# Up-projection of a hybrid decoder layer: weight sums T1, T3 and T4 of chunks 1 and 2 formed by accumulating transfers instead of on VectorE

## The reference

```
def conv_glu_ffn(h, w_up, conv_w, conv_b, w_down):
    u = h @ w_up                      # (512, 2048) @ (2048, 2 * 5632)
    c = causal_depthwise_conv(u, conv_w, width 3) + conv_b
    gate, val = jnp.split(c, 2, axis=-1)
    return (jax.nn.gelu(gate, approximate=True) * val) @ w_down
```

## Time and profile before

| | us |
|---|---|
| median of 3 runs | 2002.81 |
| lowest, highest | 2002.68, 2005.13 |
| profiled execution, its own time | 2000.05 |
| its span | 1998.1 |
| TensorE busy | 1966.3 (98%) |
| VectorE busy | 1475.0 (74%) |
| ScalarE busy | 1012.6 (51%) |
| GpSimd busy | 55.1 (3%) |

### The profile page before, as it was taken

How to read it: one execution, slowest core, us unless ns; L and a number is a source line. 1 busy time by engine, 2 the same in 40 slices (tenths; PEclk the granted TensorE clock), 3 DMA queues, 4 the chain that set the end, 5 groups by cost and what they waited for, 6 DMA issues and landing times.

```text
span 1998.1 us, 27810 instructions
## 1 busy us (share of the span) xinstructions
PE 1966.3 (98%) x10408; PEld 1678.4 (84%) x10408; DVE 1475.0 (74%) x2044; ACT 1012.6 (51%) x1539; POOL 55.1 (3%) x65
## 2 busy tenths in 40 slices
PE   8999999999999999999999999999999999999998
PEld 6888888888887889888888888888889887888786
DVE  4343544445436899788888888888888998889888
ACT  6442323435435764555555555555555655555454
POOL 0000000000000000000000000000000000000000
PEclk9999999999999999999999999999999999999999
DMA  9462322221646534777877787887786997877675
GB/s 383 147 223 94 102 90 64 85 64 64 241 133 200 185 121 162 195 194 209 230 198 198 216 228 192 205 227 210 200 207 193 310 323 233 276 244 242 214 265 202
DMA packets 229108, 388.02 MB, mean 194 GB/s; under 512 B 11842, under 2 KB 139970, under 8 KB 219120
## 3 DMA queue, kind: packets, MB, share of 16 engines
q1 hardware_dynamic: 219520, 320.19, 47.8%
q0 software_dynamic: 8208, 59.77, 14.9%
q10 hardware_dynamic: 1248, 6.29, 0.8%
HBM read 286.30 MB, written 44.07 MB: 165 GB/s over the span
## 4 chain that ended last, share of the span: by engine, by line
PE 85%; DVE 9%; issue 2%; ACT 2%; DMA 0%; DVEq 0%; ACTq 0%
PE ring L2514 15%; PE ring L2270 13%; PE ring L2272 12%; PE ring L2271 12%; PE ring L2516 8%; PE side L2514 7%; PE side L2516 3%; DVE w_lo L1906 3%; PE side L2270 3%; PE side L2271 2%; PE side L2272 2%; PE side L2346 1%; PE side L2319 1%; DVE f L2116 1%; PE side L2329 1%
## 5 line engine op out<-in xcount | busy, mean ns | idle before, releaser
L1605 DVE TENSOR_TENSOR w_lo<-raw,w_hi 128x512 fp32r<-128x512 f32 x256 | 169.5, 688 | 270.5 <-ACT w_hi L1122 270.3
L2514 PE MATMUL ring<-s,w_hi 128*128 128x512 f32 x864 | 306.2, 397 | 2.3 <-ACT snaps L1441 2.2
L1906 DVE TENSOR_TENSOR w_lo<-raw,w_hi 128x1024 fp32r<-128x1024 f32 x216 | 253.3, 1173 | 74.4 <-ACT w_hi L1332 55.9
L1906 DVE TENSOR_TENSOR w_lo<-q,w_hi 128x1024 fp32r<-128x1024 f32 x218 | 255.4, 1172 | 44.0 <-ACT w_hi L1332 27.1
L1122 ACT ACTIVATE w_hi<-raw 128x512 fp32r<-128x512 f32 x256 | 151.1, 622 | 198.2 <-PE ring L2272 193.8
L2516 PE MATMUL ring<-s,w_lo 128*128 128x256 f32 x864 | 242.0, 280 | 0.0
L1332 ACT ACTIVATE w_hi<-q 128x1024 fp32r<-128x1024 f32 x176 | 185.1, 1055 | 51.6 <-PE side L2516 46.0
L2514 PE MATMUL ring<-a,w_hi 128*128 128x512 f32 x576 | 202.6, 396 | 0.0
L2270 PE MATMUL ring<-w_hi,act_hi 128*128 128x512 f32 x488 | 193.0, 395 | 9.2 <-DVE w_lo L1605 8.7
L2514 PEld LDWEIGHTS ring<-s,w_hi 128*128 128x128 f32 x864 | 162.0, 188 | 44.3 <-ACT snaps L1441 6.2
L1332 ACT ACTIVATE w_hi<-raw 128x1024 fp32r<-128x1024 f32 x130 | 135.1, 1056 | 112.4 <-DVE raw L1609 78.4
(11 more groups left out here) (331 smaller groups left out, 4360.0 us busy)
## 6 DMA issues: line engine op xcount, KB each, us to landing
q<-in_w_up SPq DMA_DIRECT2D x65, 1024.0 KB, 5.4
raw<-in_w_in SPq DMA_DIRECT2D x24, 1024.0 KB, 5.2
raw<-in_w_up SPq DMA_DIRECT2D x23, 1024.0 KB, 8.3
q<-q POOLq DMA_DIRECT2D x19, 1024.0 KB, 6.9
q<-raw POOLq DMA_DIRECT2D x19, 1024.0 KB, 6.9
raw<-q POOLq DMA_DIRECT2D x19, 1024.0 KB, 7.3
q<-in_w_down SPq DMA_DIRECT2D x66, 256.0 KB, 4.7
raw<-in_w_down SPq DMA_DIRECT2D x66, 256.0 KB, 4.4
```

The lines of the kernel that those rows point to most:

```text
L1605: dve.tensor_tensor(w_lo[:, s, q], raw[:, s, q], w_hi[:, s, q].bitcast(F32), ALU.subtract).then_inc(lo_done, 1)
L1906: dve.tensor_tensor(lo, src, hi.bitcast(F32), ALU.subtract).then_inc(hp_lo_done, 1)
L2514: pe.matmul(bank.rearrange("p (h n) -> p h n", h=2), b_hi, hi_lo, start=first, stop=False, skip_group_check=True)
```

## The change

`PAIRED` keeps its meaning for the products. A new constant `ADDED = 1` takes its place where the sums are concerned: from chunk 1 on, T1, T3 and T4 are accumulating transfers, so six additions of 128 x 2048 leave VectorE and six 1 MB transfers join GpSimd's queue. T2 of chunk 1 stays in `after(14)`; T2 of chunk 2 moves from `after(27)`, behind that window's remainder, to `after(28)`, ahead of it. Waits for T1, T3 and T4 of chunks 1 and 2 (`t_ready`) now name the transfers' semaphores, and so does SyncE's wait for T4 of chunk 1 ahead of the load of b11 of chunk 3.

```
+ADDED = 1
 def t_count(c, name):
-    if c < PAIRED[0]:
-        order = ("T1", "T3", "T2", "T4") if c == 0 else ("T1", "T2", "T3", "T4")
+    if c < ADDED:
+        order = ("T1", "T3", "T2", "T4")
         return 4 * c + order.index(name) + 1
-    return 4 * PAIRED[0] + c - PAIRED[0] + 1
+    return 4 * ADDED + c - ADDED + 1
 def t_ready(c, name):
-    if c >= PAIRED[0] and name != "T2":
-        return {"T1": t1_in, "T3": t3_in, "T4": t4_in}[name], 16 * (c - PAIRED[0] + 1)
+    if c >= ADDED and name != "T2":
+        return {"T1": t1_in, "T3": t3_in, "T4": t4_in}[name], 16 * (c - ADDED + 1)
...
-            for c in range(PAIRED[0], CHUNKS):
+            for c in range(ADDED, CHUNKS):
                 pool.wait_ge(hp_lo_done, place(c, P1, 1) + 1)
                 pool.wait_ge(*b_landed("12", c))
                 pool.dma_start(b11_at(c)[:, :, :].rearrange("p k n -> p (k n)"),
                                b12_at[:, :, :].rearrange("p k n -> p (k n)"), accum_op=ALU.add).then_inc(t1_in, 16)
                 pool.wait_ge(*b_landed("22", c))
-                pool.wait_ge(t1_in, 16 * (c - PAIRED[0] + 1))
+                pool.wait_ge(t1_in, 16 * (c - ADDED + 1))
                 pool.dma_start(b12_at[:, :, :].rearrange("p k n -> p (k n)"),
                                raw[:, 0, :], accum_op=ALU.add).then_inc(t3_in, 16)
...
                 if w == 14:
                     make_t(1, "T2")
-                if PAIRED[0] <= c < CHUNKS and s == 0:
+                if ADDED < c < CHUNKS and s == 0:
                     make_t(c, "T2")
...
-                if w == 13:
-                    make_t(1, "T1")
-                if w == 16:
-                    make_t(1, "T3")
...
-                    if s == 5 and c < PAIRED[0]:
+                    if s == 5 and c < ADDED:
                         make_t(c, "T4")
-                    if c == 1 and s in (12, 13):
-                        make_t(c + 1, ("T1", "T2")[s - 12])
-                    if c == 2 and s == 0:
-                        make_t(c, "T3")
```

## The result

The changed kernel takes 2007.44 us (median of 16 runs, 2005.0 to 2012.24); the kernel before, run beside it, 2002.96 us (16 runs, 2000.57 to 2005.64). The ratio is 1.0025, with a 95% interval from 1.0018 to 1.0032: 4.5 us slower, where +3.2 us was forecast. The interval leaves no doubt that the kernel is slower. The time is inside the forecast's range. Run again among the experiments, the same kernel gave 1.0033 and 1.0025.

What follows compares the result with a forecast made beforehand. TensorE, busy 98% of the span, was taken to bound the kernel. The terms +1.4 + 1.7 - 0.3 + 0.4 gave +3.2 us, so 2002.81 + 3.2 = 2006.0 us, range 2001.2 to 2008.0.

Steps and rivals of the forecast that it cites:

- What can be won: Chunks 1 and 2: TensorE loses 2.3 us in all at products 18, 20 and 34, the most the change can gain.
- T2 of chunk 1, "+1.4 us, by the row of a real meeting": Ahead of product 18: T1's transfer and b22's load slow each other, so T2 starts near 732.05, 1.4 us later.
- The upper end, +2.0: Ahead of product 18: b22's load served only behind T1 lands at 732.5, T2 starts at 732.65, 2.0 us later.
- The clock, +1.7: At product 18: a 3.0 us wait brings TensorE's clock to half speed for about 3.4 us, losing 1.7 us.
- Product 20, -0.3: Chunk 1: with T3 off VectorE the combination is done some 2 us earlier, gaining 0.3 us.
- Product 34, +0.4: Chunk 2: between 0.3 us gained and 1.2 lost if spilled sums push T1 back; the middle, 0.4 us lost.
- T3 and T4 of both chunks at nothing: Chunks 1 and 2: these transfers land before their first users need them, costing nothing.
- The transfers hide: Chunk 1: T1 and b22's load do not slow each other; sum -1.5 us, 2001.3 us; chance 10%.
- the clock stays up: Product 18: its longer wait brings no fall of the clock; sum +1.5 us, 2004.3 us; chance 22%.
- VectorE holds GpSimd's transfers up: Issue of T1: VectorE's additions delay the transfer's preparation by up to 2.3 us; sum +5.5, 2008.3 us; chance 3%.
- Served one after the other: Chunks 1 and 2: meeting transfers queue whole, b22 behind T1, T1 behind spills; sum +4.6, 2007.4 us; chance 18%.
- Same, 74%: Whole kernel: 74% chance that the time stays within 0.2%, 4.0 us, of the kernel before.

Runs made afterwards that it cites:

- the kernels that have only the good half of the change: Changed kernel with T1 of chunk 1, or of chunks 1 and 2 (two forms), back on VectorE: ratio 1.0000, and 0.9995 and 0.9997.
- first profile: The changed kernel as first measured and profiled, against the kernel before: 2007.44 us, ratio 1.0025.
- third: The changed kernel run once more without edit, the later of two repeats: 2007.57 us, ratio 1.0025.
- chunk 1 alone: Changed kernel with all four sums of chunk 2 on VectorE, transfers only in chunk 1: 2008.3 us, ratio 1.0029.
- with filling matmuls: Changed kernel with 24 further matmuls between products 17 and 18 into a free bank: 2008.66 us, ratio 1.0025.
- second: The changed kernel run once more without edit, the earlier of two repeats: 2009.23 us, ratio 1.0033.

## Why the prediction was off

The direction, the range and the path by which T2's delay reaches TensorE were right. One term was too small, and the picture of the meeting behind it was wrong.

The forecast took the earlier trace rows as two transfers that share the engines and lose 2.1 us each. The list of DMA queues of the kernel before, from 1136 to 1141.5 and from 1141.5 to 1144.6, says otherwise:

```profile
q0 software_dynamic: 128, 1.05, 99.9%
...
q1 hardware_dynamic: 988, 1.00, 92.2%
```

The load, issued at 1139.80, moved nothing until all of T4 was through. By the usual microsecond from issue to first data it could have begun near 1140.8, so T4 cost it only some 0.7 us; at product 18 the load lost over 2 us in the same way. The rest of its 7.0 us is its end: from 1144.8 to 1146 the engines were busy by a share of 0.07, as at the late b12 above. T4's landing after 9.4 us came 3 us after its last data, and why is not shown.

- **What can be won.** Right: TensorE waited for about 2 us in these chunks, and the kernels that have only the good half of the change are 0.6 to 1.5 us better on the trace there and unmeasurable in the runs.
- **T2 of chunk 1, "+1.4 us, by the row of a real meeting"**: this is the term that was too small. It counted T2's start as 9.55 us behind T1's issue (722.5 to 732.05), from a T4 that met a load issued 4.8 us behind it, read as two that share the engines. Measured it is 11.0 (first profile), 11.1 (third), 11.5 (chunk 1 alone), 11.3 (with filling matmuls) and 12.8 (second). The first profile hid this, since b12 landed early there and T1 was issued 1.0 us sooner than the forecast supposed: 721.47 + 11.0 gives nearly the forecast 732.05. With b12's landing at 6.2 and 6.5 us, the duration that the forecast itself took from the earlier trace rows, T2 was 3.2 and 4.9 us late, beyond the upper end of +2.0.
- **The upper end, +2.0**, had the right mechanism and was too small as well. It let T1's data run to 6.1 us after its issue, and b22 land 3.9 us after that. Measured in the five profiles where T1 went in first, b22's first data came 7.0 to 7.6 us after T1's issue (T1's own ran to between 6.5 and 7 us, then nothing moved for 0.3 to 0.5 us), and b22 landed 3.6 to 5.2 us later. The 5.2 us are from the profile with the latest T1, where the next load, b11 of chunk 2, issued at 728.5, took its share; the end had left it out.
- **In the runs.** The delays of T2 in the three profiles of the changed kernel are 1.5, 1.7 and 4.9 us, and T1 of chunk 3 is late by 2.9, 3.0 and 7.0, a mean of 4.3. The three medians say 4.5, 6.5 and 4.8 us. A mixture of executions with an early and a late b12 gives what the runs show within their intervals (about 1.5 to 2.5 us to each side), but that is argued from few profiles, and it isn't the only reading: the changed kernel's profiles also took 713.8, 715.4 and 716.0 us from T1 of chunk 3 to T1 of chunk 21, against 712.2 and 713.6 before, and the kernel with chunk 1's transfers alone lost 5.6 us in an execution with an early b12. How the part of the loss beyond 2.9 us splits between the two is not shown.
- **The clock, +1.7**: right. It fell with every wait ahead of product 18 of 2.2 us and more, and with none of 1.57 us. Against the 23.10 us that products 18 to 26 take without a fall it cost 1.4 to 1.6 us, and 2.3 us (25.38) in the profile with the latest b22, where it stayed at 0.50 for 5 us.
- **Product 20, -0.3**: right, its gap is gone in the first profile. **Product 34, +0.4**: measured +0.1. T2 of chunk 2 came 11.10 us behind product 26 where it was 10.28 before, and the wait for the copy rose from 0.21 to 0.32 us.
- **T3 and T4 of both chunks at nothing**: right; the kernels that keep them as transfers are level with before.
- **The rivals.** *The transfers hide* and *the clock stays up* are ruled out for the changed kernel. *VectorE holds GpSimd's transfers up*: nothing of it; T3 was issued at 732.58 inside T2 (732.47 to 734.76) in 0.87 us. *Served one after the other* has the right mechanism in chunk 1: the load stood until T1 was through. In chunk 2 it was the spills that stood and not T1, so its second meeting cost nothing; that its time, 2007.4 us, is the measured one owes something to chance. The Trainium skill, *DMA: Bandwidth & Descriptors*, section "Queues, rings and completion order", has each engine take turns between the queues it has work for, a whole packet at a time. That the two transfers don't hide in each other's gaps is so. Turns are not what the traces show: from 726 to 728 T1 moved 48 packets and the load, by then 1.1 us and more behind its issue, none, and in the other order the load moved 0.92 MB before T1 moved anything. Both moved at once only for about 1 us there. Why is not shown by any run.
- **Same, 74%**: the term above was 0.1, 0.3 and 3.5 us short in the three profiles, 1.3 us on the mean, and the forecast stood 0.8 us from the bound of 4.0 us. The measured 4.5 us is beyond it, by less than its own interval.

**Still open.** The stretch from chunk 3 to chunk 21 took 712.2 to 714.9 us in the five profiles in which neither T2 of chunk 1 nor product 34 was late (a mean of 714.0) and 713.8 to 717.2 in the nine others (a mean of 715.6). It may be chance in so few, or a late start may carry a little further, though the latest start of all (+7.3 us, T1 issued later) had only 713.9; the time is lost in single chunks, 0.5 to 2 us at a time, beside waits for the `snap` copy. No run isolates it.

## What to carry to other kernels

Before work is moved from an engine to the DMA queues, look not only at what the transfer takes alone, but at the loads issued in its 7 to 8 us: here one that stood on the path paid 2.5 to 6 us for a sum that VectorE had made in 2.3 us out of its spare time. A row of "a meeting" is worth little without its lead and without the bytes of each queue, window by window: two landings that are both late look like sharing, and here were one transfer behind the other. Take the order of issue and the data that each has still to move, and ask for the transfer behind them too. And where a new step hangs on a landing that had slack before, look at how that landing scatters over several executions, since the one profiled may show the kind one.

## What the runs showed of the hardware

- An accumulating transfer of 1 MB within SBUF moved as 128 packets in 5 to 5.5 us (190 to 210 GB/s), from some 1.3 to 1.6 us after its issue on. A 1 MB load issued 1.8 to 3.4 us behind it moved its first data only 0.3 to 0.5 us after the transfer's last, and took 7.4 to 10.8 us instead of 4.9; spills of 128 KB issued 1.1 to 2.6 us behind one took 6.3 and 7.2 us instead of 2.3 and 2.5. With the load issued 0.6 us ahead, the load took 5.7 us and the transfer 11.2.
- One and the same 1 MB load, issued at the same place of the kernel, landed after 4.9 to 5.5 us in six executions and after 5.9 to 6.5 in eight. The eight ended with 0.8 to 1.4 us in which the engines were busy by a share of 0.06 to 0.07, about one of the 16; in the six this lasted 0.4 us at most.
- TensorE's granted clock fell to 0.50 (1.2 GHz) with waits of 2.2 to 7.8 us ahead of product 18 and stayed at 1.00 (2.4 GHz) with waits of 1.57; matmuls that cut a wait of 3.9 us down to 0.53 kept it up, and products 18 to 26 took 1.4 us less.
